# An encoder step on one core: a shorter list of requests in the opening, projection stores issued by SP, and two schedules respaced

## The reference

```
every layer:  h = RMSNorm(x) * (1 + scale(c)) + shift(c);  x = x + gate(c) * mixer(h)
layer 0:  qa, ka, va, fa, ga, qb, kb, vb, iq, ik, iw, gb = split(h @ w_in)
          branch A: softmax attention with a forget gate (8 heads of 64)
          branch B: rotary q, k (8 heads); a query sees only the keys that an indexer selects:
             rel = relu(iq . ik) per index head; score = sum over heads of iw * rel; top-k of score
          x += gate * (concat(A * silu(ga), B * silu(gb)) @ w_out)
layer 1:  latent attention (16 heads): q from a normalised latent of 384, keys and values from a
          normalised latent of 128, a rotary key of 32 shared by the heads, silu gate, w_out
outputs:  final RMSNorm of x, and the new rows of k, v, log f, index k, latent and rotary key
```

## Time and profile before

| | |
|---|---|
| median of 3 runs | 1937.97 us (1937.79 to 1943.93) |
| profiled execution | 1940.82 us |
| its span, first to last instruction | 1939.1 us |
| mean granted TensorE clock, share of full speed | 0.94 |
| PE, DVE, ACT, POOL busy | 1689.8, 1297.3, 941.7, 209.0 us |

### The profile page before, as it was taken

How to read it: one execution, slowest core, us unless ns; L and a number is a source line. 1 busy time by engine, 2 the same in 40 slices (tenths; PEclk the granted TensorE clock), 3 DMA queues, 4 the chain that set the end, 5 groups by cost and what they waited for, 6 DMA issues and landing times. The chain is left out here.

```text
span 1939.1 us, 34317 instructions
## 1 busy us (share of the span) xinstructions
PE 1689.8 (87%) x12754; PEld 1314.9 (68%) x12754; DVE 1297.3 (67%) x2825; ACT 941.7 (49%) x1897; POOL 209.0 (11%) x310
## 2 busy tenths in 40 slices
PE   3794789999998966899998998889996999999798
PEld 0572458888877854677776787677774776676687
DVE  0553577878999934678888655553365777777764
ACT  2422552227211364577876225447644676777421
POOL 2001100010000002101010000000004222221000
PEclk7797899999999987899998998989997999999899
DMA  9366511432233119968774643232235111111432
GB/s 347 116 211 191 121 39 51 130 105 88 74 98 107 62 55 223 227 195 217 198 197 147 230 172 119 70 110 96 73 79 117 28 28 45 27 28 51 152 130 98
DMA packets 229550, 235.17 MB, mean 121 GB/s; under 512 B 139350, under 2 KB 164214, under 8 KB 227339
## 3 DMA queue, kind: packets, MB, share of 16 engines
q1 hardware_dynamic: 222506, 213.07, 38.3%
q0 software_dynamic: 6880, 19.92, 2.8%
HBM read 173.98 MB, written 58.95 MB: 120 GB/s over the span
## 5 line engine op out<-in xcount | busy, mean ns | idle before, releaser
L274 PE MATMUL PS<-ab_wh,hT 128*128 128x512 f32 x576 | 231.4, 402 | 5.7 <-DVE ab_wl L694 5.7
L275 PE MATMUL PS<-ab_wl,hT 128*128 128x512 f32 x576 | 227.3, 395 | 0.0
L276 PE MATMUL PS<-ab_wh,hT 128*128 128x512 f32 x576 | 226.6, 393 | 0.0
L1191 DVE TENSOR_SCALAR_CACHE_REDUCE topk_junk<-scores,topk_small 128x528 bf16<-128x528 f32 (+6 forms) x224 | 194.6, 916 | 1.3
L2368 DVE CUSTOM_DVE_ANT_0 la_S<-PS,la_mask 128x128 f32<-128x128 f32 (+3 forms) x144 | 107.5, 747 | 41.5 <-PE PS L276 28.5
L274 PEld LDWEIGHTS PS<-ab_wh,hT 128*128 128x128 f32 x576 | 109.4, 190 | 29.2 <-ACT ab_wh L618 3.9
L276 PEld LDWEIGHTS PS<-ab_wh,hT 128*128 128x128 f32 x576 | 109.2, 190 | 25.0
L1541 ACT ACTIVATE at_P<-at_S,at_nm 128x128 f32<-128x128 f32 (+2 forms) x144 | 110.5, 767 | 29.5 <-DVE at_nm L1586 29.3
L275 PEld LDWEIGHTS PS<-ab_wl,hT 128*128 128x128 f32 x576 | 109.3, 190 | 22.1
L274 PE MATMUL PS<-out_wh,out_mT 128*128 128x512 f32 x288 | 116.1, 403 | 4.7 <-DVE out_mT L1844 4.7
L2290 ACT ACTIVATE la_P<-la_S,la_nm 128x128 f32<-128x128 f32 (+3 forms) x144 | 110.4, 767 | 9.3 <-DVE la_nm L2368 9.2
(11 more groups left out here) (424 smaller groups left out, 4437.3 us busy)
## 6 DMA issues: line engine op xcount, KB each, us to landing
mod_ada_w<-in_ada_w SPq DMA_DIRECT2D x16, 1024.0 KB, 6.6
ab_wl_raw<-in_ab_w_in SPq DMA_DIRECT2D x64, 256.0 KB, 4.8
out_g<-scratch_gates_nat SPq DMA_DIRECT2D x18, 512.0 KB, 5.3
mod_ada_w<-in_ada_w SPq DMA_DIRECT2D x16, 512.0 KB, 5.0
at_kc<-in_cache_a_k SPq DMA_DIRECT2D x8, 1024.0 KB, 8.9
at_vc<-in_cache_a_v SPq DMA_DIRECT2D x8, 1024.0 KB, 7.5
at_kc<-in_cache_b_k SPq DMA_DIRECT2D x8, 1024.0 KB, 7.7
at_vc<-in_cache_b_v SPq DMA_DIRECT2D x8, 1024.0 KB, 5.3
```

The source lines that it names most:

```text
L274: nc.tensor.matmul(out, x[0], w[0], start=start, stop=False)
L275: nc.tensor.matmul(out, x[0], w[1], start=False, stop=False)
L276: return nc.tensor.matmul(out, x[1], w[0], start=False, stop=stop)
L1191: go(V.tensor_scalar(mark, x, limit, 0.0, op, ALU.add, accum_out=cnt[:, m:m + 1]), 0 if m == M - 1 else 1)
```

## The change

- The opening's SP ends after `fetch_weights`. The tables, the three side pieces and the forget bias are requested at the head of the ix projection's SP program (`fetch_tables`), and DVE waits for the long tables at its first rope.
- ACT splits the first five (`EARLY`) of ix's weight tiles at the end of the opening. In ix it splits the other three after the first tile of rows; DVE splits three before and five after (four and four before).
- In `projection`, the natural stores are issued by SP: at step s, behind the turned store of step s - 4, it waits for the rows of step s and stores them. POOL has no program there any more.
- In `index_scores` the samples' batches come four steps apart, with turning at 10 + 4b, high half 11 + 4b, scoring 15 + 4b, relu 16 + 4b, sum 19 + 4b (6, 7, 9, 10, 11 + 5b before); the sample queries are split at step 9 (5 before); the new keys are scored at step 42, their relu is at 44 and their sum at 46.
- `selection` spreads the passes by the kind of step: about 4.34 per copy step, 3.95 per silu step and 1.97 per rope step, the last at step 70 (four a step to step 64 before).

```diff
@@ opening, SP
             entry.fetch_weights(sp)
-            sp.dma_start(c.ropeC[:], c.i["rope_cos"].rearrange("(i p) d -> p i d", p=P)).then_inc(rope_in, 16)
-            sp.dma_start(c.ropeS[:], c.i["rope_sin"].rearrange("(i p) d -> p i d", p=P)).then_inc(rope_in, 16)
-            for n in range(AW):
-                sp.wait_ge(w_used, KT - AW + n + 1)
-                entry.side.load(sp, n)
-            sp.dma_start(c.ropeCs[:], c.i["rope_cos_short"].rearrange("(i p) d -> p i d", p=P)).then_inc(entry.tables_in, 16)
-            sp.dma_start(c.ropeSs[:], c.i["rope_sin_short"].rearrange("(i p) d -> p i d", p=P)).then_inc(entry.tables_in, 16)
-            sp.dma_start(c.fbias[:], dram(c.i["ab_f_bias"], 0, [[0, P], [1, H]])).then_inc(entry.tables_in, 16)
-            sp.wait_ge(rope_in, 32)
@@ opening, ACT
+            for k in range(EARLY):
+                entry.split_high(act, k)
@@ projection, SP
-            sent = [0, 0]
+            if side:
+                front.fetch_tables(sp)
+            sent, stored = [0, 0], [0] * 4
             for s in range(len(steps) + LAG + 1):
...
+                if s < len(steps) and groups[steps[s][0]].nat:
+                    g, i = steps[s]
+                    sp.wait_ge(nat_done, s + 1)
+                    for part, src in groups[g].nat(i, nat[:, s % 4, :]):
+                        sp.dma_start(part, src).then_inc(nat_out[s % 4], 16)
+                        stored[s % 4] += 16
@@ projection, POOL (the whole program)
-            for s, (g, i) in enumerate(steps):
-                if groups[g].nat:
-                    pool.wait_ge(nat_done, s + 1)
-                    for d, src in groups[g].nat(i, nat[:, s % 4, :]):
-                        pool.dma_start(d, src).then_inc(nat_out[s % 4], 16)
-                        counts[s % 4] += 16
@@ projection, ACT
-            ahead = 0 if front and front.SPLIT else groups[0].kt
-            for k in range(ahead // 2 if front else ahead):
+            for k in range(0 if front else groups[0].kt):
                 split_high(0, k)
             for i in range(2 if front else 0):
                 front.act(act, i)
                 if i == 0:
-                    for k in range(ahead // 2, ahead):
+                    for k in range(front.HIGH, groups[0].kt):
                         split_high(0, k)
@@ projection, DVE
                     if kind == "rope":
+                        if side and s == 0:
+                            dve.wait_ge(front.rope_in, 32)
@@ index_scores
-    turn_at, score_at, sum_at = {6 + 5 * b: b for b in range(NB)}, {9 + 5 * b: b for b in range(NB)}, {11 + 5 * b: b for b in range(NB)}
-    high_at, relu_at = {7 + 5 * b: b for b in range(NB)}, {10 + 5 * b: b for b in range(NB)}
-    NEW_ROW = 12
+    at = lambda first: {first + 4 * b: b for b in range(NB)}
+    turn_at, high_at, score_at, relu_at, sum_at = at(10), at(11), at(15), at(16), at(19)
+    NEW_ROW, NEW_KEYS, NEW_RELU, NEW_SUM = 12, 42, 44, 46
@@ selection
+ROOM = {"copy": 4.4, "silu": 4.0, "rope": 2.0}
+    room = [ROOM[g.kind] for g in groups for _ in range(NT)]
+    until = lambda s: math.ceil(topk.passes() * sum(room[:s + 1]) / sum(room[:-1]))
-        for _ in range(-(-topk.passes() // (n - 2)) if s < n - 1 else topk.passes()):
+        for _ in range(until(s) - (until(s - 1) if s else 0) if s < n - 1 else topk.passes()):
             next(work[0], None)
```

More of the change, by code:

```diff
@@ L9 @@
+import math
 import numpy as np
@@ L399, in enter, with fetch_tables @@
     def enter(self, stack):
-        super().enter(stack)
-        self.wh = stack.enter_context(self.nc.sbuf_tensor("ix_wh0", [P, KT, 512], F32R))
+        pass
+    def fetch_tables(self, sp):
+        c, by_tile = self.c, lambda n: self.c.i[n].rearrange("(i p) d -> p i d", p=P)
+        sp.dma_start(c.ropeC[:], by_tile("rope_cos")).then_inc(self.rope_in, 16)
+        sp.dma_start(c.ropeS[:], by_tile("rope_sin")).then_inc(self.rope_in, 16)
+        for n in range(AW):
+            self.side.load(sp, n)
+        sp.dma_start(c.ropeCs[:], by_tile("rope_cos_short")).then_inc(self.tables_in, 16)
+        sp.dma_start(c.ropeSs[:], by_tile("rope_sin_short")).then_inc(self.tables_in, 16)
+        sp.dma_start(c.fbias[:], dram(c.i["ab_f_bias"], 0, [[0, P], [1, H]])).then_inc(self.tables_in, 16)
     def wait_rows(self, pe, i):
@@ L694, in split_low @@
                 nc.vector.tensor_tensor(wl[slot(g)][:, k, 0:n], raw[slot(g)][:, k, 0:n], wh[slot(g)][:, k, 0:n], ALU.subtract).then_inc(w_lo, 1)
-            ahead = 0 if front and front.SPLIT else groups[0].kt
-            for k in range(ahead // 2 if front else ahead):
+            first_low = 0 if front and front.SPLIT else front.LOW if front else groups[0].kt
+            for k in range(first_low):
                 split_low(0, k)
@@ L701, in _ @@
                 front.dve(dve, i)
-                if i == 0:
-                    for k in range(ahead // 2, ahead):
+                if i == 0 and not front.SPLIT:
+                    for k in range(first_low, groups[0].kt):
                         split_low(0, k)
@@ L1002, in sum_sample, with score_new @@
                 weighted(b, 6, PAST, rs[:, b % 2, :]).then_inc(sum_done, 1)
[L1004 to L1020, removed]
-                                                    start=d == 0, stop=d == 1)
-                    last.then_inc(mm_done, 1)
+            def score_new():
+                pe.wait_ge(kc_lo, NB)
+                for b in range(NB):
+                    qb = [qs[:, d, b].rearrange("d h t -> d (h t)") for d in range(2)]
+                    last = product(nc, PS[:, 4, b * TS:(b + 1) * TS], qb, [kn[:, d, b * TS:(b + 1) * TS] for d in range(2)], True, True)
+                last.then_inc(new_done, 1)
@@ new lines, in sum_new @@
+            def sum_new():
+                pe.wait_ge(new_read, 1)
+                pe.wait_ge(tr_read, 3)
+                for b in range(NB):
+                    last = weighted(b, 7, TS, rs_new[:, b, :])
+                last.then_inc(new_sum, 1)
+            for s in range(N):
+                i, h = steps[s]
+                m = s // H
+                if s == 0:
+                    pe.wait_ge(k_done, 1)
+                if i * P == 512 and h == 0:
+                    pe.wait_ge(k_done, 2)
+                if s >= 2:
+                    pe.wait_ge(relu_done, s - 1)
+                if h == 0:
+                    pe.wait_ge(q_done, m + 1)
+                n = (i + 1) * P
+                for a in range(0, n, 512):
+                    w = min(512, n - a)
+                    for d in range(2):
+                        last = nc.tensor.matmul(PS[:, 2 * (s % 2) + a // 512, 0:w], q[:, m % 3, h, :], k[:, d, a:a + w],
+                                                start=d == 0, stop=d == 1)
+                last.then_inc(mm_done, 1)
@@ L1031, in _ @@
                     sum_sample(sum_at[s])
-            pe.wait_ge(kc_lo, NB)
-            for b in range(NB):
-                qb = [qs[:, d, b].rearrange("d h t -> d (h t)") for d in range(2)]
-                last = product(nc, PS[:, 4, b * TS:(b + 1) * TS], qb, [kn[:, d, b * TS:(b + 1) * TS] for d in range(2)], True, True)
-            last.then_inc(new_done, 1)
-            pe.wait_ge(new_read, 1)
-            pe.wait_ge(tr_read, 3)
-            for b in range(NB):
-                last = weighted(b, 7, TS, rs_new[:, b, :])
-            last.then_inc(new_sum, 1)
+                if s == NEW_KEYS:
+                    score_new()
+                if s == NEW_SUM:
+                    sum_new()
         @block.scalar
@@ L1057, in _ @@
             nc.scalar.activation(row_p[:], PS[0:H, 4:6, :].rearrange("p a b -> p (a b)"), ACT.Copy).then_inc(tr_read, 1)
-            for s in range(N + 1):
-                if s < N:
-                    act.wait_ge(mm_done, s + 1)
-                    if s >= 3:
-                        act.wait_ge(acc_done, s - 2)
-                    n = (steps[s][0] + 1) * P
-                    nc.scalar.activation(rel[:, s % 3, 0:n], flat(2 * (s % 2), n), ACT.Relu).then_inc(relu_done, 1)
-                if s == 5:
+            for s in range(N):
+                act.wait_ge(mm_done, s + 1)
+                if s >= 3:
+                    act.wait_ge(acc_done, s - 2)
+                n = (steps[s][0] + 1) * P
+                nc.scalar.activation(rel[:, s % 3, 0:n], flat(2 * (s % 2), n), ACT.Relu).then_inc(relu_done, 1)
+                if s == 9:
                     act.wait_ge(s_in, 16 * 5)
@@ L1239, in steps, with selection @@
             yield
-def selection(nc, c):
+ROOM = {"copy": 4.4, "silu": 4.0, "rope": 2.0}
+def selection(nc, c, groups):
     tiles = [(QT, TOPK_S)] + [(i, TOPK_P) for i in SELECT_TILES]
     topk = TopK(nc, c, semaphore(nc, "topk_link"), tiles)
+    room = [ROOM[g.kind] for g in groups for _ in range(NT)]
+    until = lambda s: math.ceil(topk.passes() * sum(room[:s + 1]) / sum(room[:-1]))
     work = []
@@ L2500, in build @@
```

(2 more changed lines are left out.)

25 lines of the change are left out of this document (13 added, 12 removed).

## The result

| | before | changed |
|---|---|---|
| median of the runs | 1939.26 us (4 runs, 1937.79 to 1943.93) | 1922.24 us (4 runs, 1917.40 to 1924.23) |
| profiled execution | 1940.82 us | 1917.40 us |
| ratio | | 0.9904, 95% interval 0.9877 to 0.9932 |

The change makes the kernel 0.96% faster: by the ratio, which goes by the runs' means, 18.6 us of 1939, with an interval of 13 to 24 (the medians are 17.0 apart). The profiled execution of the changed kernel is the fastest of its four runs and that of before lies above its median, so the two traces differ by 23.4, more than the kernels do.

The account below looks back on a forecast made before the run. TensorE is busy 87% of the span, so time can be won only where PE waits. Terms 10.4 + 0.4 - 2 + 4 + 6 + 1 - 4 = 15.8 us; 1937.97 - 15.8 = 1922, forecast range 1917 to 1928, all bounds 1906 to 1939.

Parts of the forecast that it names:

- 1, opening and head: Opening and head of ix: moved requests win 10.4 us, hidden by DMA engines only 8% busy; respaced splits win 0.4.
- 2, ix: ix block: ada_w load 10 stands behind a natural store on SP's queue, everything behind comes late; costs 2 us.
- 3, index_scores: index_scores: PE's waits for turned keys and last sums go, less query copies and new keys' products; wins 4 us.
- 4, ab: ab block: respread passes end group 6 15 us earlier, finishing passes lengthen the last gate; wins 6 us net.
- 4, gap: After ab's last gate: some 5 us before SP's next request may hang on POOL's queue; 0 to 4, taken as +1.
- 5, c: c block: weight loads for q0, second gate and two more q fall behind natural stores; costs 4 us.
- (a): Opening's gain comes back where ada_w loads set the pace or first rope waits for tables; 1931 to 1934, chance 0.13.
- (b): SP's in-order queue becomes the bound in c, losing more than 25.6 us there; slower, 1944, chance 0.08.
- (c): Finishing passes eat the ab gain and the relu loop the index_scores gain, both 0; 1932, chance 0.11.
- (d): PE-bound to the end: the ab passes give 11 us and the boundary behind 4; 1914, chance 0.18.
- (e): Ring order: a store on SP's queue waits behind a train of weight loads; 1925, counted within the forecast's 0.50.

Follow-up runs that it names:

- the lag: The changed kernel, but SP issues the natural store of step s-1 at step s instead of that of step s; ratio 0.9911.
- gate_light: The changed kernel with natural stores of ix and c back on POOL and the last gate's room 2.5 a step, not 4.0 (fewer passes); ratio 0.9830.
- opening_only: The kernel before with only the opening's change: requests moved out, early splits, respaced splits of the head; ratio 0.9944.
- scores_only: The kernel before with only the respaced index_scores of the change; ratio 0.9994, stage 94.6 us.
- pool_all: The changed kernel with all natural stores (ix, ab and c) back on POOL; ratio 0.9929.
- sp_ab_only: The changed kernel with the natural stores of ix and c back on POOL, those of ab on SP; ratio 0.9884, median 1913.7 us.
- c_hoist_late: The changed kernel with c's loads for gate 1 and the last q requested at the ninth step of the gate group ahead; ratio 0.9892.
- c_hoist: The changed kernel with c's loads for gate 1 and the last q requested at the seventh step of the gate group ahead; ratio 0.9913.

## Why the prediction was right, and where it was not

That the time came out at 1922.24 for a forecast of 1922 is in part luck. The gap gave 4.1 more than its term, and ix, index_scores and c together gave 6.0 less than theirs; the terms as measured add up to 13.4, which from 1939.26 would be 1925.9, and no part of the change accounts for the other 3.6. Terms by the stages' means over the kernels with and without each part:

| term | predicted | measured | from |
|---|---|---|---|
| 1, opening and head | +10.8 | +10.9 | first product 66.6 (four kernels), 55.7 (ten) |
| 2, ix | -2 (-0.5 to -4) | -3.8 | 116.9 with POOL, 120.7 with SP, 117.0 with the lag |
| 3, index_scores | +4 (0 to 7) | +2.0 | 95.1 (four), 93.1 (ten, 90.4 to 94.6) |
| 4, ab | +6 (2 to 11) | +5.4 | 15.4 less 10.0 |
| 4, gap | +1 (0 to 4) | +5.1 | 8.1 and 3.0 |
| 5, c | -4 (-0.5 to -8) | -6.2 | 362.7 (nine kernels with POOL's stores in c), 368.9 in the changed kernel |
| sum | +15.8 | +13.4 | interval of the whole: 13 to 24 |

1. Right, in place and size: the block ended 0.5 behind modT, and the 8% of the earlier trace rows covered the requests. (Between the two traces the first product moved by 12.4; 1.5 of that is modT itself, written earlier by code that the change leaves alone.)
2. Right in mechanism, and inside its bounds. The size was off by the train of loads: PE waited at load 10 for 4.10 and at each load behind it, and the last multiplication came 109.9 after the first product in place of 106.0.
3. The waits went as said, 6.9 to 1.4, though the one that is left is longer than the 0.5 that the prediction allowed. What was won is less. PE, at 21.23 of 22, seems to have had less idle time than the moved products and the query copies took; no run takes these apart. The clock, which the prediction didn't price here, is the larger spread.
4. The step held by its own numbers: the end of group 6 was to come 15 earlier and came 15.4 earlier; 53 us were worked out for the last gate from its first row on, 55.0 came (646.55 to 701.55), and DVE held it. That those passes could leave the gate at no cost was missed, and it is worth twice the term (gate_light).
   The gap is the step that failed: "If they hang on POOL's queue they go: 0 to 4, I take +1". They do, and 5.1 went, above the bound. The "some 5 no row names" are POOL's DRAIN of 4.46, which the trace of before holds and the prediction didn't look up; with it the gap adds up: 0.30 to the store's issue, 2.29 until it lands, 0.27 to the DRAIN, 4.46, and 0.77 to the request. The changed kernel has 0.03, 2.00, 0.26, 0.01 and 0.72.
5. Right in mechanism, three places as named. The krope steps and q0 cost 2.0 (2 predicted), the second gate's weights 1.9 (1.5); the last q's cost 2.3 (0.5, at most 1), because they came 20 late: SP used to be three rows ahead of the gate. The one that waited for weights was ACT; PE's own waits in c name none.

The rivals: (a) fell with opening_only; (b), SP's queue as the bound, is what parts 2 and 5 cost, but c lost 6.2 of the 25.6 at which it would decide; (c) did not come for part 4, as DVE reached group 7 on time, and its half on part 3 nearly came in scores_only; (d) came half, by the gap; (e), the ring: the gate stores' median landing is 2.0 on SP's queue against POOL's 2.3, the longest of all 99 natural stores lands in 7.0 against 6.7 before, well under the 13 of the prediction, and in neither kernel does an engine wait for a natural buffer. The rule on ring order that the prediction weighed (the Trainium skill, "DMA: Bandwidth & Descriptors", Queues, rings and completion order) costs nothing here.

What stays open: the whole-kernel ratios have intervals of 0.4 to 0.6%, so the stores alone (-3.8 + 5.1 - 6.2 = -4.9 by stages) are not confirmed by the times: the changed kernel at 0.9904 and pool_all at 0.9929 overlap, and their middles even stand the other way round. sp_ab_only, some 10 better than the changed kernel by ix and c, is 3.9 better by the ratios (0.9884), also within the intervals. What decides which way the clock goes, and why a DRAIN takes longer with every store, stays open too.

## What to carry to other kernels

When stores move to another engine's in-order queue, list for each of its requests how many steps ahead of the stored rows it runs today: that look-ahead, more than the time to issue a store, is what is lost. Moving the loads ahead of the stores helps only where the loads' own condition is already met (c_hoist_late); where it isn't, the stores wait for the load (c_hoist). Work given to an engine's idle time should be spread by what each piece costs there, and the stage that ends the block should get the least. Where GpSimd issues a block's stores and the block ends on one of them, look for its DRAIN, and give the last store to another engine, so that the DRAIN runs beside it.

## What was not expected of the hardware

- GpSimd's DRAIN at the end of a block took about 0.08 for each store that it had issued there (0.80 after 9, 2.99 after 36, 4.38 after 53, 4.46 after 54), behind the landing of the last one. So a block whose last store is issued by GpSimd goes on 7.8 after that store's issue, one that ends on a store of SyncE 3.0, or 3.7 where GpSimd issued the 53 ahead of it (the stores themselves land in 2.3 and 2.0). The Trainium skill ("DMA: Bandwidth & Descriptors", Latency and other measured facts) gives about 1 us to the first byte on GpSimd's path and 0.6 on SyncE's; 0.3 between the landings is near that. What is left is the DRAIN.
- Unchanged code differs by up to 6 us, and the differences go with the granted clock. Branch A, 129.6 us of it before and 129.5 after the change, in windows of both:

```profile
730.40:860.00 129.60, 104.11 (x1317) 79.08 (x1318) 79.30 (x194) 75.58 (x184) 25.17 (x43) 0.85 0.88 216
```

```profile
710.50:840.00 129.50, 104.37 (x1390) 81.19 (x1403) 85.00 (x206) 81.07 (x195) 25.20 (x43) 0.90 0.96 225
```

  PE did 1390 products at a clock of 0.90 and 1317 at 0.85 in the same time. Over the 14 kernels the mean clock of the whole branch is 0.87 to 0.89 in the five where it takes under 145, and 0.85 in the three where it takes over 150. A stage's length compared between two traces is worth no more than its spread over kernels that share the stage.
